# A prologue that loads modulation chunks in pairs, into eight places, and modulates and projects tile by tile

## The chip, the core and the metric

The kernel runs on one core of one Trainium2 chip. The metric is the device time of one execution in microseconds (us); what is compared are medians of several runs. The core has five engines that work side by side and wait for each other by semaphores: TensorE (PE in the profile), VectorE (DVE), ScalarE (ACT), GpSimd (POOL), and SyncE (SP), which here only issues DMAs.

## The reference

Two blocks of two layers each act on 512 tokens of 1024 values; the first block also carries 256 context tokens, so 768 columns in all. The change touches only the start of the first layer of the first block:

```
silu_c = silu(c);  silu_cc = silu(c_ctx)
mod = silu @ ada_w[0] + ada_b[0]          # 6 vectors of 1024: shift1, scale1, gate1, ...
u = rms_norm(h, g_mix[0]) * (1 + scale1) + shift1     # tokens with c, context with c_ctx
q, k, v = split(u @ na_wqkv)              # 16 heads of 64
q, k = rms_norm(q, gain_q), rms_norm(k, gain_k)
y = neighborhood_attention(q, k, v, ...) @ na_wo
```

Everything is float32. Shift1 and scale1 are two of the six vectors; the other four are needed later.

## The kernel before

**Layout.** Tokens stand transposed in SBUF: 8 tiles of 128 features (k = 0 to 7) by 768 columns, 512 tokens (w = 0) and 256 context tokens (w = 1). Weights come from one tensor `stream` in chunks of 128x2048 float32, 1 MB each. A product of float32 precision is made of three matmuls (`mm3`, lines 287 to 289): each operand is split into a high part, made by ScalarE, and a low part, the rest, made for weights by GpSimd (`low_part`, L248, four pieces of 512 columns a chunk) and for activations by VectorE (L547).

**Stages.** The program is a row of stages, each one `nc.Block()` with a program for each engine. At the end of a block all five engines wait for each other, SyncE too; I call the instant at which the next block's first instructions go the boundary.

**The prologue (first block).** SyncE issues the small tensors, the tokens h in two halves, chunks 0 to 3 of the modulation weights into four places, the first attention weight chunk (queries and keys of head pair 0, "qk0") into `w_raw`, and then chunks 4 to 7, each when the place four chunks earlier has been read. Chunks 0 to 3 hold the shift and 4 to 7 the scale, 256 features each. For each chunk TensorE makes rows (`mod_rows`, 8 matmuls, L564), VectorE copies them (`row`, L687) and TensorE turns them into columns (`mod_columns`, 4 matmuls, L571). Meanwhile ScalarE and VectorE make 1/rms of every token (squares L414, sums L433, Ln and Exp L416 and L419). Only with all eight chunks in columns does VectorE add the bias (`mod`) and make the gain (`gsc`); that ends the block. ScalarE and GpSimd split qk0 during it.

**The attention stage (`na_stage`, second block).** SyncE's program begins with the weights of the values ("vv0", two DMAs, L1505), then 24 small DMAs of bias tables (L1513), then the next weight chunk, the queries and keys of head pair 1 ("qk1", L1501). VectorE and ScalarE modulate 16 pieces (8 tiles of 512 columns, 8 of 256; `Apply`: scale L538, high L522, low L547), and TensorE follows tile by tile with the first queries and keys (`qk_first`: 8 tiles, two products each, 48 matmuls of 512 columns). Then come, in program order:

```
TensorE: sums(0,0), qk(0,2), sums(0,1), sums(0,2), values(0,0), values(0,1), values(0,2), scores(0), ...
ScalarE: square(0,0), square(0,1), rstd(0,0), high(vv0), square(0,2), high(qk1), rstd(0,1), rstd(0,2), ...
```

`qk(0,2)` projects the context, `sums` adds squares, `rstd` reads those sums out of PSUM, `high` splits a weight chunk that has landed. All results of projections and sums go in turn through two PSUM banks (`Linear`): result number n may be written when result n-2 has been read. `values(0,0)` is number 6; number 4 is `sums(0,1)`, which `rstd(0,1)` reads. It also needs the low part of vv0 from GpSimd.

Of the kernel before, what the change touches and what calls it, by code (L numbers as in the profile page):

```python
# [495 lines left out]
class Apply:  # L496
# [3 lines left out]
    def __init__(self, m, rstd, tok, gain, shift, tmp, by_columns=False):  # L500
        self.m, self.rstd, self.gain, self.shift, self.tmp = m, rstd, gain, shift, tmp
        self.by_columns = by_columns
        self.items = [(k, a, b, w) for a, b, w in spans(tok) for k in range(KT)]
        self.scaled, self.high, self.low = (m.shared("norm_" + x) for x in ("scaled", "high", "low"))
        for x in ("scaled", "high", "low"):
            m.spent("norm_" + x, len(self.items))

    def ready(self, k, w=0):
        return self.low.at(KT * w + k + 1)
# [14 lines left out]

    def dve(self, dve):
        m = self.m

        def scale(n):
            k, a, b, w = self.items[n]
            if n >= len(self.tmp):  # L530
                dve.wait_ge(*self.low.at(n - len(self.tmp) + 1))
            late = len(self.rstd.shape) == 3
            out, h, rstd = self.place(n), m.h[:, k, a:b], self.rstd if late else self.rstd[:, a:b]
            if late:
                out, h = quarters(out), quarters(h)
            if self.by_columns and w == 0:
                out, h, rstd = columns_as_rows(out), grid(h), grid(rstd)
            dve.scalar_tensor_tensor(out=out, in0=h, scalar=self.gain(k, w), in1=rstd, op0=ALU.mult,  # L538
                                     op1=ALU.mult).then_inc(self.scaled.sem)

        def low(n):
            k, a, b, w = self.items[n]
            dve.wait_ge(*self.high.at(n + 1))
            if self.shift is None:
                ins = dve.tensor_tensor(m.ul[:, k, a:b], self.place(n), m.uh[:, k, a:b].bitcast(F32), ALU.subtract)
            else:
                ins = dve.scalar_tensor_tensor(out=m.ul[:, k, a:b], in0=self.place(n), scalar=self.shift(k, w),  # L547
                                               in1=m.uh[:, k, a:b].bitcast(F32), op0=ALU.add, op1=ALU.subtract)
            ins.then_inc(self.low.sem)

        scale(0)
        for n in range(len(self.items)):
            if n + 1 < len(self.items):
                scale(n + 1)
            low(n)
# [37 lines left out]
def prologue(nc, m):  # L593

    A, D, E = m.A, m.D, m.E
    FIRST = 8
    with ExitStack() as ctx:
# [3 lines left out]
        more = sb("ada_more", [P, 3, CHUNK])  # L601
        landed = m.ada_ring_in = [m.sem(f"ada_ring_in{s}") for s in range(4)]
        slots = [m.raw[:, 1, :]] + [more[:, n, :] for n in range(3)]
        m.vec_in, h_in, rest_in = m.sem("vec_in"), m.sem("h_in"), m.sem("h_rest_in")
        vec_in = m.vec_in
        pmod = m.bank[:, 6, 0:4 * FIRST]
        norm = Norm(m, sb("n_sq", [P, 2, TOK]), sb("n_acc", [P, TOK]), m.rstd, TOK)
        A.plan(["exp_c"] + Norm.act_steps + ["exp_lam", "w0_hi"])
        D.plan(["eps", "zero", "sig1", "sig2", "silu", "sel"] + Norm.dve_steps + ["row0", "row1", "row2", "row3"] +
               ["q1", "q2", "q3", "lam1", "lam2"] + [f"row{c}" for c in range(4, FIRST)] + ["mod", "gsc"])  # L610
        E.plan(["ada0", "ada1", "n_sum", "lamdot"] + [f"ada{c}" for c in range(2, FIRST)] + ["columns"])
        m.G.plan(["w0_lo"])

        with nc.Block() as block:
            @block.sync
            def _(sp):
# [4 lines left out]
                for c in range(FIRST):  # L621
                    if c == 4:
                        sp.dma_start(m.raw[:, 0, :], m.stream[N_ADA]).then_inc(m.first_in, 16)
                    if c >= 4:
                        sp.wait_ge(E.sem, E.at(f"ada{c - 4}"))
# [3863 lines left out]
```

## Time and profile before

| | us |
|---|---|
| three runs | 2732.64, 2738.05, 2738.17 (median 2738.05) |
| span of the profiled execution, first to last instruction | 2732.2 |
| TensorE busy in it | 2622.8 (96%) |
| boundary between prologue and attention stage (first DMA of the stage) | 40.84 |
| first matmul of `values(0,0)` | 69.84 |

The profiled execution has no time of its own in the list of runs; the nearest of the three, 2732.64, is 0.4 us above its span, and the median 5.9 us above. In a timeline a row gives start, duration, engine, line, operation and tiles; a bracket says how long the engine was idle before it and what ended that. A line of a helper stands for all who call it. For DMAs the row gives the issue, and "to landing" the time from the issue until the data are there.

### The profile page before, as it was taken

The page shows a single profiled execution, that of the slowest core. Times are in us where ns is not written, and L with a number is a line of the kernel's source. Part 1 is how long each engine was busy: PE and PEld are TensorE (multiplying, and loading weights), DVE is VectorE, ACT ScalarE, POOL GpSimd, SP SyncE. Part 2 cuts the span into 40 slices and gives each one's busy share as a digit, 9 for nine tenths or more (in the row PEclk, how much of TensorE's full clock was granted, in tenths as well). Part 3 has the DMA queues.
Part 4 walks back from the last instruction along what each step waited for, and adds up shares of the span by engine and source line. Part 5 has one row for each costly group of instructions (what it writes and reads, how often), then busy time and mean ns, then how long its engine had stood idle before and what let it go on. Part 6 is the DMA issues. An engine that isn't in the chain of part 4 may idle for free. (4 is left out here: it accounts for less than half of the span.)

```text
span 2732.2 us, 38254 instructions
## 1 busy us (share of the span) xinstructions
PE 2622.8 (96%) x14748; PEld 2130.9 (78%) x14748; DVE 1546.6 (57%) x2893; ACT 1073.3 (39%) x1864; POOL 875.4 (32%) x651
## 2 busy tenths in 40 slices
PE   6899999999999999999889999999999999999997
PEld 4777786788888888766668888787778888788886
DVE  4434344687777778556664444544556445516555
ACT  4454545422222222565542322344553434542222
POOL 1211121243333333021124444333334333444443
PEclk8999999999999999999999999999999999999999
DMA  6323333223332332110012222322212221222221
GB/s 244 116 79 97 107 99 115 85 96 108 106 107 107 108 108 70 57 47 32 32 47 96 104 92 92 96 66 74 78 47 102 71 85 62 94 93 93 93 93 62
DMA packets 69652, 243.02 MB, mean 89 GB/s; under 512 B 11780, under 2 KB 29700, under 8 KB 49288
## 3 DMA queue, kind: packets, MB, share of 16 engines
q1 hardware_dynamic: 69512, 241.15, 25.8%
q8 instruction: 89, 1.46, 0.2%
q14 instruction: 51, 0.42, 0.0%
HBM read 239.02 MB, written 2.10 MB: 88 GB/s over the span
## 5 line engine op out<-in xcount | busy, mean ns | idle before, releaser
L248 POOL TENSOR_TENSOR w_lo<-w_raw,w_hi 128x512 fp32r<-128x512 f32 x612 | 820.2, 1371 | 1736.7 <-ACT w_hi L241 602.9
L287 PE MATMUL bank<-u_hi,w_hi 128*128 128x512 f32 (+1 forms) x1952 | 731.8, 375 | 10.8 <-DVE u_lo L547 5.0
L289 PE MATMUL bank<-u_hi,w_lo 128*128 128x512 f32 (+1 forms) x1952 | 719.4, 369 | 0.0
L288 PE MATMUL bank<-u_lo,w_hi 128*128 128x512 f32 (+1 forms) x1952 | 718.7, 368 | 0.0
L287 PEld LDWEIGHTS bank<-u_hi,w_hi 128*128 128x128 f32 x1952 | 368.9, 189 | 80.9 <-issue 14.0
L288 PEld LDWEIGHTS bank<-u_lo,w_hi 128*128 128x128 f32 x1952 | 368.9, 189 | 62.2 <-issue 2.5
L289 PEld LDWEIGHTS bank<-u_hi,w_lo 128*128 128x128 f32 x1952 | 368.5, 189 | 62.3
L1052 DVE SCALAR_TENSOR_TENSOR resid<-bank,mod,resid 128x512 f32<-128x512 f32 (+1 forms) x384 | 242.0, 657 | 140.5 <-PE bank L289 136.1
L287 PE MATMUL bank<-hid_hi,w_hi 128*128 128x512 f32 (+1 forms) x768 | 275.5, 359 | 0.0
L289 PE MATMUL bank<-hid_hi,w_lo 128*128 128x512 f32 (+1 forms) x768 | 273.0, 355 | 0.0
L288 PE MATMUL bank<-hid_lo,w_hi 128*128 128x512 f32 (+1 forms) x768 | 272.1, 354 | 0.0
L241 ACT ACTIVATE w_hi<-w_raw 128x2048 fp32r<-128x2048 f32 x64 | 122.7, 1917 | 299.0 <-PE bank L289 298.0
L287 PE MATMUL bank<-w_hi,u_hi 128*128 128x256 f32 (+1 forms) x624 | 193.9, 311 | 5.3 <-POOL w_lo L248 3.0
L763 DVE SCALAR_TENSOR_TENSOR ada_acc<-ada_ring,silu_c,ada_acc 128x256 f32<-128x256 f32 x336 | 195.6, 651 | 0.0
L289 PE MATMUL bank<-w_hi,u_lo 128*128 128x256 f32 (+1 forms) x624 | 190.9, 306 | 0.0
L288 PE MATMUL bank<-w_lo,u_hi 128*128 128x256 f32 (+1 forms) x624 | 190.8, 306 | 0.0
L913 ACT ACTIVATE relu<-bank 128x768 f32<-128x768 f32 (+1 forms) x64 | 45.2, 706 | 319.6 <-PE bank L289 319.6
L289 PEld LDWEIGHTS bank<-hid_hi,w_lo 128*128 128x128 f32 x768 | 144.8, 189 | 23.7
L288 PEld LDWEIGHTS bank<-hid_lo,w_hi 128*128 128x128 f32 x768 | 144.2, 188 | 22.2
L287 PEld LDWEIGHTS bank<-hid_hi,w_hi 128*128 128x128 f32 x768 | 144.1, 188 | 20.8
L1039 DVE TENSOR_TENSOR square<-relu 128x768 f32<-128x768 f32 (+1 forms) x64 | 63.7, 996 | 143.1 <-ACT relu L913 142.9
L287 PEld LDWEIGHTS bank<-w_hi,u_hi 128*128 128x128 f32 x624 | 119.8, 192 | 17.7 <-POOL w_lo L248 4.6
(410 smaller groups left out, 3888.6 us busy)
## 6 DMA issues: line engine op xcount, KB each, us to landing
w_raw<-stream SPq DMA_DIRECT2D x150, 1024.0 KB, 4.9
w_raw<-stream SPq DMA_DIRECT2D x56, 512.0 KB, 4.4
ada_ring<-stream SPq DMA_DIRECT2D x48, 512.0 KB, 4.7
bias<-bias SPq DMA_DIRECT2D x192, 64.0 KB, 2.3
ada_more<-stream SPq DMA_DIRECT2D x6, 1024.0 KB, 13.2
resid<-h SPq DMA_DIRECT2D x2, 1536.0 KB, 8.7
w_raw<-stream SPq DMA_DIRECT2D x8, 256.0 KB, 3.9
out<-resid SPq DMA_DIRECT2D x8, 256.0 KB, 2.0
```

The source lines that it names most:

```text
L241: act.activation(m.wh[:, s, 0:width], m.raw[:, s, 0:width], ACT.Copy).then_inc(m.hi_split, 1)
L248: ins = eng.tensor_tensor(m.wl[:, s, w], m.raw[:, s, w], m.wh[:, s, w].bitcast(F32), ALU.subtract)
L287: pe.matmul(out, lh, rh, start=start, stop=False)
L288: pe.matmul(out, lh, rl, start=False, stop=False)
L289: return pe.matmul(out, ll, rh, start=False, stop=stop)
L763: ins = dve.scalar_tensor_tensor(out=acc, in0=w[:, k, :], scalar=scale, in1=acc, op0=ALU.mult, op1=ALU.add)
L913: act.activation(relu[:, par, t, :], place(g, t)[:, 0:tok], ACT.Relu).then_inc(*A.mark(f"e_{g}{t}"))
L1039: dve.tensor_tensor(square[:, t, :], relu[:, par, t, :], relu[:, par, t, :], ALU.mult).then_inc(*D.mark(f"s_{g}{t}"))
L1052: ins = dve.scalar_tensor_tensor(out=m.h[:, n, a:b], in0=place(g, n)[:, a:b], scalar=m.mod[:, layer, 5, n, w:w + 1], in1=m.h[:, n, a:b], o ...
```

## The change

The eight chunks get a place each (seven in `ada_more`, one in `w_raw`), so SyncE issues all of them without a wait, and in pairs: shift and scale of the same 256 features. The qk0 chunk goes behind the first pair. As soon as a pair is in columns, VectorE makes `mod` and `gsc` for those two tiles and modulates them, with ScalarE, into four buffers `scaled`; TensorE projects their queries and keys. The modulation of all 16 pieces and the whole of `qk_first` thus stand in the prologue's block, and the attention stage begins with `sums(0,0)` on TensorE and `square(0,0)` on ScalarE. SyncE's program of the attention stage is the same. The core of the diff:

```diff
         self.by_columns = by_columns
         self.items = [(k, a, b, w) for a, b, w in spans(tok) for k in range(KT)]
+        if order:
+            self.items = [self.items[KT * w + k] for k, w in order]
+        self.index = {(k, w): n for n, (k, a, b, w) in enumerate(self.items)}
...
         for x in ("scaled", "high", "low"):
             m.spent("norm_" + x, len(self.items))
 
     def ready(self, k, w=0):
-        return self.low.at(KT * w + k + 1)
+        return self.low.at(self.index[k, w] + 1)
 
     def place(self, n):
...
+    def scale(self, dve, n):
+        m = self.m
+        k, a, b, w = self.items[n]
+        if n >= len(self.tmp):
+            dve.wait_ge(*self.low.at(n - len(self.tmp) + 1))
...
     A, D, E = m.A, m.D, m.E
-    FIRST = 8
+    FIRST, QUADS = 8, KT // 2
...
-        more = sb("ada_more", [P, 3, CHUNK])
+        more = sb("ada_more", [P, FIRST - 1, CHUNK])
...
+        chunks = [s * QUADS + q for q in range(QUADS) for s in range(2)]
+        pmod = [m.bank[:, 4 + q, 0:8] for q in range(QUADS)]
...
+        tmp = sb("scaled", [P, 4, LAT])
+        apply = Apply(m, m.rstd, TOK, lambda k, w: m.gsc[:, 0, 0, k, w:w + 1],
+                      lambda k, w: m.mod[:, 0, 0, k, w:w + 1], [tmp[:, n, :] for n in range(4)], by_columns=True,
+                      order=[(2 * q + x, w) for q, w in ((0, 0), (0, 1), (1, 0), (1, 1), (2, 0), (3, 0), (2, 1), (3, 1))
+                             for x in range(2)])
+        m.qk_first_done = m.sem("na_lin_done")
...
-                for c in range(FIRST):
-                    if c == 4:
+                for n, c in enumerate(chunks):
+                    if n == 2:
                         sp.dma_start(m.raw[:, 0, :], m.stream[N_ADA]).then_inc(m.first_in, 16)
-                    if c >= 4:
-                        sp.wait_ge(E.sem, E.at(f"ada{c - 4}"))
-                    sp.dma_start(slots[c % 4], m.stream[c]).then_inc(landed[c % 4], 16)
+                    sp.dma_start(slots[n], m.stream[c]).then_inc(landed[n], 16)
...
                 act.wait_ge(m.first_in, 16)
                 act.activation(m.wh[:, 0, :], m.raw[:, 0, :], ACT.Copy).then_inc(*A.mark("w0_hi"))
+                apply.act(act)
...
+                def columns(q):
+                    if q == 3:
+                        pe.wait_ge(A.sem, A.at("exp_lam"))
+                    for s in range(2):
+                        pe.wait_ge(D.sem, D.at(f"row{2 * q + s}"))
+                        ins = mod_columns(pe, m, pmod[q][:, 4 * s:4 * s + 4], part[:, s, :])
+                    ins.then_inc(*E.mark(f"columns{q}"))
+
+                def qk_first(q):
+
+                    wh, wl = (w[:, 0, :].rearrange("p (k n) -> p k n", k=KT) for w in (m.wh, m.wl))
+                    for k in range(2 * q, 2 * q + 2):
+                        pe.wait_ge(*apply.ready(k))
+                        for p in range(2):
+                            c = slice(p * P, p * P + P)
+                            ins = mm3(pe, m.bank[:, p, :], wh[:, k, c], wl[:, k, c], m.uh[:, k, 0:LAT],
+                                      m.ul[:, k, 0:LAT], k == 0, k == KT - 1)
+                            if k == KT - 1:
+                                ins.then_inc(m.qk_first_done)
...
                 columns(0)
-                for c in range(2, FIRST):
-                    rows(c)
-                    columns(c - 1)
-                columns(FIRST - 1).then_inc(*E.mark("columns"))
+                for q in range(1, QUADS):
+                    rows(2 * q)
+                    rows(2 * q + 1)
+                    columns(q)
+                    if q == 1:
+                        pe.wait_ge(m.G.sem, m.G.at("w0_lo"))
+                    qk_first(q - 1)
+                qk_first(QUADS - 1)
...
+                def row(n):
+                    dve.wait_ge(E.sem, E.at(f"ada{n}"))
+                    if n >= 2:
+                        dve.wait_ge(E.sem, E.at(f"columns{n // 2 - 1}"))
+                    dve.tensor_copy(part[:, n % 2, :], m.bank[:, 2 + n % 2, 0:2 * P]).then_inc(*D.mark(f"row{n}"))
...
+                row(0)
+                row(1)
...
-                for c in range(4, FIRST):
-                    row(c)
-                dve.wait_ge(E.sem, E.at("columns"))
...
+
+                def normed(q, w):
+                    n = apply.index[2 * q, w]
+                    apply.scale(dve, n)
+                    apply.scale(dve, n + 1)
+                    apply.lower(dve, n)
+                    apply.lower(dve, n + 1)
+                for q in range(QUADS):
+                    modulation(q)
+                    normed(q, 0)
+                    if q + 1 < QUADS:
+                        row(2 * q + 2)
+                        row(2 * q + 3)
+                    if q < 2:
+                        normed(q, 1)
+                normed(2, 1)
+                normed(3, 1)
...
-        norm = Apply(m, m.rstd, TOK, lambda k, w: m.gsc[:, 0, 0, k, w:w + 1],
-                     lambda k, w: m.mod[:, 0, 0, k, w:w + 1],
-                     [pt[:, 0, :], pt[:, 1, :], s_sb[:, :, :].rearrange("p h n -> p (h n)")], by_columns=True)
...
-                norm.act(act, 0, KT + 4)
                 square(0, 0)
                 square(0, 1)
-                norm.act(act, KT + 4)
                 rstd(0, 0)
                 high(fills[1])
                 square(0, 2)
...
-                norm.dve(dve)
                 for p in range(QK):
                     normalise_qk(0, p)
                 maximum(0)
...
-                def qk_first():
-
-                    pe.wait_ge(*chunk_lo.at(fill["qk", 0] + 1))
-                    wh, wl = columns(("qk", 0), 0), columns(("qk", 0), 1)
-                    for k in range(KT):
-                        pe.wait_ge(*norm.ready(k))
...
                         for k in range(KT):
-                            if i == 0 and x == 0:
-                                pe.wait_ge(*norm.ready(k, 1))
...
-                qk_first()
                 sums(0, 0)
                 qk(0, 2)
```

TensorE before, in the prologue: rows of one chunk (`ada_more`, or `w_raw` for its place) and columns of the one before (`parts`) in turn.

```order
L564 MATMUL bank<-ada_more,silu_c 32x256 [waits vector_steps,ada_ring_in3]
L564 MATMUL bank<-ada_more,silu_c 32x256 x7
L571 MATMUL bank<-mod_sel,parts 128x2 [waits vector_steps]
L571 MATMUL bank<-mod_sel,parts 128x2
L564 MATMUL bank<-w_raw,silu_c 32x256 [waits vector_steps,ada_ring_in0]
L564 MATMUL bank<-w_raw,silu_c 32x256 x7
L571 MATMUL bank<-mod_sel,parts 128x2 [waits vector_steps]
L571 MATMUL bank<-mod_sel,parts 128x2
```

Each chunk's columns stand behind the next chunk's rows, and nothing else waits between them. TensorE now, from the columns of the second pair on. `gpsimd_steps` is the low part of qk0, `late_norm_low` the low part of a modulated tile, `ada_first_in4` and `5` the landing of the third pair.

```order
L574 MATMUL bank<-mod_sel,parts 128x2 [waits vector_steps]
L574 MATMUL bank<-mod_sel,parts 128x2
L287 MATMUL bank<-u_hi,w_hi 128x512 [waits late_norm_low,gpsimd_steps]
L288 MATMUL bank<-u_lo,w_hi 128x512
L289 MATMUL bank<-u_hi,w_lo 128x512
...
L289 MATMUL bank<-u_hi,w_lo 128x512
L567 MATMUL bank<-ada_more,silu_c 32x256 [waits vector_steps,ada_first_in4]
L567 MATMUL bank<-ada_more,silu_c 32x256 x7
L567 MATMUL bank<-ada_more,silu_c 32x256 [waits vector_steps,ada_first_in5]
L567 MATMUL bank<-ada_more,silu_c 32x256 x7
```

The twelve matmuls of two tiles, and their waits, now stand ahead of the rows of the third pair.

VectorE before, from the first copies of rows (`parts<-bank`) to the first modulated tile (`pt` and `s` are its buffers, `resid` is h):

```order
L687 COPY parts<-bank 128x256 [waits tensor_steps] x4
L692 TENSOR_SCALAR vec_sb<-vec_sb 128x1 x3
L695 TENSOR_TENSOR misc<-lam 128x1 [waits scalar_steps]
L698 TENSOR_SCALAR misc<-misc 128x1 [waits vector_steps]
L687 COPY parts<-bank 128x256 [waits tensor_steps] x4
L704 TENSOR_TENSOR mod<-bank,vec_sb 128x32 [waits tensor_steps]
L708 SCALAR_TENSOR_TENSOR gsc<-mod,vec_sb 128x16 [waits vector_steps]
...
L1697 UNCONDITIONAL_BRANCH [waits barrier_Pool_Activation_PE_DVE_SP_release]
L538 SCALAR_TENSOR_TENSOR pt<-resid,gsc,rstd_first 128x8x64 x2
L547 SCALAR_TENSOR_TENSOR u_lo<-pt,mod,u_hi 128x512 [waits late_norm_high]
```

The modulation followed all eight copies and the boundary. VectorE now, from the first `mod` to the second:

```order
L730 TENSOR_TENSOR mod<-bank,vec_sb 128x2x4 [waits tensor_steps]
L733 SCALAR_TENSOR_TENSOR gsc<-mod,vec_sb 128x4 [waits vector_steps]
L539 SCALAR_TENSOR_TENSOR scaled<-resid,gsc,rstd_first 128x8x64 [waits scalar_steps,vector_steps]
L539 SCALAR_TENSOR_TENSOR scaled<-resid,gsc,rstd_first 128x8x64
L549 SCALAR_TENSOR_TENSOR u_lo<-scaled,mod,u_hi 128x512 [waits late_norm_high] x2
L723 COPY parts<-bank 128x256 [waits tensor_steps] x2
L539 SCALAR_TENSOR_TENSOR scaled<-resid,gsc,rstd_first 128x256 x2
L549 SCALAR_TENSOR_TENSOR u_lo<-scaled,mod,u_hi 128x256 [waits late_norm_high] x2
L730 TENSOR_TENSOR mod<-bank,vec_sb 128x2x4 [waits tensor_steps]
L733 SCALAR_TENSOR_TENSOR gsc<-mod,vec_sb 128x4 [waits vector_steps]
```

The copies of rows (`parts<-bank`) of the second pair now stand behind two modulated tiles.

## Rows read from the trace of the kernel before

**Rows 1.** The page's span; a row of TensorE's waits, 0 to 140 us: total, times, longest.

```profile
span 2732.2 us, 38254 instructions
...
PE bank L287 <- POOL w_lo L248: 1.8, 1, 1.8
```

**Rows 2.** SyncE's timeline: start, us, issuing instructions, line.

```profile
40.84 0.81 SPq L1505 DMA_DIRECT2D w_raw<-stream  x2
41.70 15.31 SPq L1513 DMA_DIRECT2D bias<-bias  x24
57.05 13.10 SPq L1501 DMA_DIRECT2D w_raw<-stream  x2
```

**Rows 3.** Line 1501 from 50 to 62 us, with its DMA's landing.

```profile
L1501 SPq DMA_DIRECT2D w_raw<-stream x1: 591/591/591, 57.0 to 57.0; - x1
...
DMA to landing us min/median/max: 6.0/6.0/6.0
```

**Rows 4.** ScalarE's timeline, 15 to 71 us.

```profile
22.41 0.15 ACT L638 ACTIVATE lam<-bank 128x2 f32<-128x2 f32 x1
...
62.85 1.90 ACT L1577 ACTIVATE w_hi<-w_raw 128x2048 fp32r<-128x2048 f32 x1
...
66.79 1.91 ACT L1577 ACTIVATE w_hi<-w_raw 128x2048 fp32r<-128x2048 f32 x1
68.59 0.69 ACT L1591 ACTIVATE qk_sq<-bank,misc 128x512 f32<-128x512 f32 x1
```

**Rows 5.** TensorE's timeline, 15 to 70 us.

```profile
22.19 0.61 PE L571 MATMUL bank<-mod_sel,parts 128*128 128x2 f32 x4
22.73 1.07 PE L564 MATMUL bank<-ada_more,silu_c 128*32 128x256 f32 x16
...
27.37 1.94 PE L564 MATMUL bank<-w_raw,silu_c 128*32 128x256 f32 x16 [3.04 <-DMA w_raw<-stream]
...
46.00 0.63 PE L289 MATMUL bank<-u_hi,w_lo 128*128 128x512 f32 x1
46.43 0.63 PE L287 MATMUL bank<-u_hi,w_hi 128*128 128x512 f32 x1
...
52.27 0.39 PE L288 MATMUL bank<-u_lo,w_hi 128*128 128x512 f32 x1
52.50 0.39 PE L289 MATMUL bank<-u_hi,w_lo 128*128 128x512 f32 x1
...
69.84 0.38 PE L287 MATMUL bank<-w_hi,u_hi 128*128 128x256 f32 x1 [1.76 <-POOL w_lo L248]
```

**Rows 6.** VectorE's timeline, 38 to 62 us.

```profile
38.39 0.42 DVE L687 COPY parts<-bank 128x256 f32<-128x256 f32 x1 [2.39 <-PE bank L564]
40.16 0.19 DVE L704 TENSOR_TENSOR mod<-bank,vec_sb 128x32 f32<-128x32 f32 x1 [1.35 <-PE bank L571]
...
40.90 2.10 DVE L538 SCALAR_TENSOR_TENSOR pt<-resid,gsc,rstd_first 128x512 f32<-128x512 f32 x2 [0.34 <-PEq L614]
...
59.49 0.49 DVE L547 SCALAR_TENSOR_TENSOR u_lo<-pt,mod,u_hi 128x256 fp32r<-128x256 f32 x1 [1.37 <-ACT u_hi L522]
...
61.74 0.48 DVE L547 SCALAR_TENSOR_TENSOR u_lo<-pt,mod,u_hi 128x256 fp32r<-128x256 f32 x1 [0.18 <-ACT u_hi L522]
```

**Rows 7.** VectorE's timeline, 62 to 76 us.

```profile
62.98 0.75 DVE L1703 SCALAR_TENSOR_TENSOR qk_normed<-qk_normed,vec_sb,qk_sq 128x512 f32<-128x512 f32 x1 [0.76 <-ACT qk_sq L1594]
69.97 1.60 DVE L1703 SCALAR_TENSOR_TENSOR qk_normed<-qk_normed,vec_sb,qk_sq 128x512 f32<-128x512 f32 x1 [6.24 <-ACT qk_sq L1594]
71.50 2.92 DVE L1708 SCALAR_TENSOR_TENSOR qk_normed<-qk_normed,vec_sb,qk_sq 128x256 f32<-128x256 f32 x2
```

**Rows 8.** GpSimd's instructions on w_lo, 63 to 76 us.

```profile
L248 POOL TENSOR_TENSOR w_lo<-w_raw,w_hi x8: 1253/1278/1727, 64.8 to 74.1; 128x512 fp32r<-128x512 f32 x8
```

**Rows 9.** Windows: stretch, length, busy per engine, granted clock, DMA share, GB/s.

```profile
34.00:36.00 2.00, 2.00 (x19) 0.95 (x11) 0.42 (x1) 0.00 (x0) 0.00 (x0) 0.50 0.07 29
70.00:80.00 10.00, 10.00 (x72) 10.00 (x73) 4.42 (x3) 2.50 (x5) 5.57 (x4) 0.83 0.64 203
```

## What is forecast, with its working

> **What bounds the kernel now.** I read the page first: the span is 2732.2 us [rows 1] and TensorE is busy for most of it, so time is won or lost only where TensorE waits or runs at its low clock. The change touches the first 70 us, so I went on to the timelines of the engines there, and then asked of each wait which of its conditions came last. Up to 34 us the stretch is a matter of DMA: in the window from 34 us on only 29 GB/s are left [rows 9], the last chunk is there. Then come copies, columns and `mod` until the boundary at 40.84 [rows 2, 6]; then VectorE modulates 16 pieces until 62.22, with TensorE behind it. The last wait is what counts. `values(0,0)` starts at 69.84, on the low part of vv0 [rows 1, 5]. From there TensorE works through the values without a pause, and everything later hangs on it by semaphores, so I take the shift of that start as the shift of the end. `values(0,0)` has three conditions: TensorE must be through with what is ahead, vv0 must be split, and `rstd(0,1)` must have read its bank. The third was close already: `rstd(0,1)` starts on ScalarE at 68.59 and takes 0.69 [rows 4], 0.6 us before the low part came. It stands behind `high(qk1)`, and that needs the DMA of qk1.
>
> **That DMA hangs on the boundary alone.** SyncE issues vv0 at 40.84, then 24 bias loads in a row, 15.31 us of issuing, and qk1 at 57.05, which is 16.2 after the boundary; it lands 6.0 us later [rows 2, 3], at boundary + 22.2. Before, nobody noticed: ScalarE came to `high(qk1)` at 66.79 [rows 4], boundary + 26.0. If the boundary moves later while the work behind it shrinks, this transfer is what ends last:
>
> values(0,0) = boundary + 22.2 (landing) + 1.8 (`high`, 66.79 to 68.59) + 0.7 (Ln) = boundary + 24.7, against boundary + 29.0 before [rows 4, 5].
>
> So the change saves 4.3 us behind the boundary, all of its earlier projection included, and costs whatever it adds in front. It breaks even with a boundary at 45.1.
>
> **Where the boundary goes.** All 16 pieces now lie in front of it on VectorE, in a block that ends only when the last is done.
> - Start. `mod` of the first pair waits for `lam`, which needs `exp_lam`, done at 22.56 [rows 4]; with the small instructions behind it 22.9.
> - The pieces took 40.90 to 62.22 less waits of 1.37 and 0.18 [rows 6]: 19.8.
> - Six copies of rows at 0.42 [rows 6]: 2.5. Four times `mod` and `gsc`; one pair with its wait took 40.16 to about 40.6 [rows 6], I take 0.5: 2.0.
> - Together 22.9 + 24.3 = 47.2, if VectorE never waited. Even this is behind 45.1.
> - GpSimd. It now splits qk0 while VectorE modulates. That chunk is third in the queue of large ones; in its place before stood one whose rows TensorE made at 22.73 or earlier [rows 5], so it is there when ScalarE comes from `exp_lam`, at 22.6, and is split by 24.5 (1.9 a chunk [rows 4]). GpSimd begins then. Before, no piece of the modulation ran beside GpSimd, but the normalising of queries did: the same instruction took 0.75 alone and 1.60 beside `w_lo`, the two of 256 columns 1.46 each where others take 0.48 [rows 6, 7]. That is 0.85 to 1.0 for each instruction that meets a GpSimd piece. Four pieces meet four: 3.4. GpSimd's pieces stretch as well, from 1.25 to 1.73 [rows 8], so qk0 is split at 24.5 + 4 x 1.73 = 31.4.
> - TensorE. It may start `qk_first` of the first pair at 31.4 only, and the rows of the third pair are queued behind these twelve matmuls. At the low clock one costs 0.43 (46.00 to 46.43), at the high 0.23 [rows 5]. The engine has been mostly idle, so 12 x 0.43 = 5.1, done at 36.5; rows of a chunk cost 1.07 or 1.94 [rows 5]. With the clock up by then they end at 37.6 and 38.7. VectorE, by the sums above, asks for them at about 36.3, and its copies lie between: it waits 2.0. For the last pair it waits for two chunks' columns (2 x 0.61 and the handing over [rows 5]): 1.3. Together 3.3.
> - The boundary itself, from `gsc` to the next block's first instructions: 0.3 [rows 2, 6].
>
> Boundary: 47.2 + 3.4 + 3.3 + 0.3 = 54.2. The last pair's chunks have landed at 34.5 and bind nothing, and `qk_first` of the last pair ends under the context pieces of 256 columns (eight instructions of up to 0.48 [rows 6], over 3 us, against six matmuls at 0.43), so neither adds. At the floor no contention and no waits leave 47.5; at the ceiling TensorE stays at its low clock through the prologue: the middle two `qk_first` cost 2.4 more each, six rows 0.87 more each, the columns 0.8 more a pair, some 11 us, of which most is on the path, since VectorE waits for the rows; boundary 63 to 65.
>
> **The rule on the shared port.** Rows 7 and 8 show both sides stretched. The Trainium skill, page "SBUF — State Buffer", section "Who interferes with whom", says that a VectorE instruction with two SBUF inputs contends with a GpSimd instruction that reads SBUF, and that the loser waits for the whole of the other's instruction. By that rule each of the four pieces would cost VectorE its full 1.25, 5.0 in all, and the boundary would be at 55.8; the trace agrees in kind, with 0.85 to 1.0 a piece.
>
> **The sum.** values(0,0) = 54.2 + 24.7 = 78.9, against 69.84: +9.1. Two small costs: TensorE is idle for some 15 us ahead of it, so the values start at the low clock. In the window of 70 to 80 it already had a mean of 0.83 [rows 9], 3.4 us at half speed, that is 1.7 lost; a second such stretch may come, from 0 to 1.7, I take 0.5. And the next chunk's DMA is now issued right behind qk1 and may slow its landing, from 0 to 1.5; I take 0.4. Nothing is saved in return: the two `sums`, the context projection and splitting vv0 all end by boundary + 14, idle behind the transfer. Forecast +10.0 us: 2742.2 for the profiled span, and on the median, 5.9 above the span, 2738.05 + 10 = 2748.0.
>
> **Rivals.**
> 1. *The clock stays low* through the prologue: boundary 63 to 65 and +19 to +21, 2758. For it: rows took 1.94 at 27.37, and in the window of 34 to 36 us the granted clock was 0.50 although TensorE was busy throughout [rows 5, 9]. Against it: in `qk_first` it rose between 46.4 and 52.3 [rows 5]. Chance 12%.
> 2. *The overlaps cost little*: no contention, short waits, boundary at 48 to 51, +3 to +6, 2742.5. For it: GpSimd may slip into VectorE's waits. Against it: rows 7. Chance 21%.
> 3. *The faster side: qk1 does not bind.* If the transfer of qk1 were hidden after all, the chain by vv0 would decide: landing no later than the 6.0 of rows 3, `high` 1.9 [rows 4], GpSimd 4 x 1.25 [rows 8], thus boundary + 12.9. With 54.2 this gives 67.1, -2.7 us; with 50 it gives -7: 2731 to 2735.3. It decides once qk1 is issued within about 5 us of the boundary instead of 16.2. For it: no engine waited for this DMA in the profile. Against it: ScalarE's order and SyncE's are the same as before, and 24 issues at 0.64 each don't shrink. Chance 6%.
> 4. *The pairs do not land as pairs.* With nine transfers queued at once they could share the engines and land together near 34 us; then VectorE starts its first tile there instead of at 23, boundary about 59, +15: 2753. Against it: with five large ones queued before, the second modulation chunk after the first pair could be used at 22.73, long before the last of them was needed [rows 5]. Chance 4%.
>
> **How the numbers follow.** The forecast has 57%. A change below 0.2%, 5.5 us, cannot be told from none. Slower: nearly all of the forecast (55), all of 1 and 4 (16), a third of 2 (7): 0.79. Same: two thirds of 2, the forecast's tail: 0.15. Faster: 0.06. Range: from case 2 (+3.5, 2741.5) to just short of case 1 (2757). The forecast's own bounds are +7 to +13.
>
> **What would show it.** Right: the block ends near 54 with VectorE last; the qk1 DMA is issued 16.2 later; ScalarE is idle for over 10 us ahead of a `w_hi` that ends in a DMA's landing; TensorE is idle as long ahead of `values(0,0)`, near 79; VectorE instructions near 25 to 31 us are stretched beside `w_lo`; VectorE waits for TensorE at the rows of the third pair. Wrong: `values(0,0)` begins within 15 us of the boundary, or the boundary lies before 47, or later stages differ by more than a microsecond in length.

## The result: 12.8 us slower, and where the profile puts it

| | before | after |
|---|---|---|
| median of four runs each | 2736.86 us (2732.64 to 2738.17) | 2749.64 us (2749.29 to 2750.15) |
| profiled execution | span 2732.2 (time not among the four) | 2749.29, span 2747.5 |
| boundary (next block's first instructions) | 40.84 | 55.76 |
| `values(0,0)` starts | 69.84 | 80.23 |
| first scores | 88.79 | 100.14 |

The ratio is 1.0044, with a 95% interval of 1.0028 to 1.006: slower by 12.0 us by the ratio, 7.7 to 16.4 by the interval. The forecast was +10.0, 2748.0. In every run that has both numbers the time is 1.8 us above the span, so I estimate the profiled execution of before at 2734.0, 2.9 below its median; that of after is 0.4 below its own. The spans therefore differ by more (15.3) than the medians (12.8).

What TensorE waited for from 0 to 140 us in the changed kernel (total us, times, longest):

```profile
PE bank L567 <- DMA w_raw<-stream: 15.2, 1, 15.2
PE bank L287 <- ACT qk_sq L1645: 14.0, 1, 14.0
PE bank L574 <- DVE parts L723: 5.0, 2, 4.0
```

In [rows 1] line 287 waited 1.8 us for GpSimd. It now waits 14.0 us, for ScalarE's Ln of `rstd(0,1)`. The first row is the start of the program, the same in both. ScalarE alone does not explain the second; read from ScalarE back to SyncE. ScalarE's timeline (start, us, instruction, what ended the idle time before it):

```profile
23.41 0.15 ACT L650 ACTIVATE lam<-bank 128x2 f32<-128x2 f32 x1
...
62.12 1.92 ACT L1631 ACTIVATE w_hi<-w_raw 128x2048 fp32r<-128x2048 f32 x1 [2.69 <-DMA w_raw<-stream]
...
77.60 1.91 ACT L1631 ACTIVATE w_hi<-w_raw 128x2048 fp32r<-128x2048 f32 x1 [12.56 <-DMA w_raw<-stream]
79.41 0.67 ACT L1645 ACTIVATE qk_sq<-bank,misc 128x512 f32<-128x512 f32 x1
```

SyncE's timeline:

```profile
55.76 0.80 SPq L1559 DMA_DIRECT2D w_raw<-stream  x2
56.62 15.93 SPq L1567 DMA_DIRECT2D bias<-bias  x24
72.59 1.05 SPq L1555 DMA_DIRECT2D w_raw<-stream  x2
```

These answer to [rows 2, 4]. SyncE's three steps are in the same order as before and nearly as long (15.93 us for the bias loads, against 15.31); what has moved is their start, with the boundary. qk1 is issued at 72.59 and has landed 5.01 us later, when ScalarE, idle for 12.56 us, takes it up; the Ln that line 287 waits for stands right behind.

The cost in front of the boundary is on VectorE's timeline:

```profile
23.86 0.16 DVE L730 TENSOR_TENSOR mod<-bank,vec_sb 128x8 f32<-128x8 f32 x1
...
24.25 2.13 DVE L539 SCALAR_TENSOR_TENSOR scaled<-resid,gsc,rstd_first 128x512 f32<-128x512 f32 x2
26.23 3.37 DVE L549 SCALAR_TENSOR_TENSOR u_lo<-scaled,mod,u_hi 128x512 fp32r<-128x512 f32 x2
...
30.19 2.23 DVE L539 SCALAR_TENSOR_TENSOR scaled<-resid,gsc,rstd_first 128x256 f32<-128x256 f32 x2
...
36.73 0.75 DVE L549 SCALAR_TENSOR_TENSOR u_lo<-scaled,mod,u_hi 128x512 fp32r<-128x512 f32 x1 [0.23 <-ACT u_hi L525]
38.96 0.42 DVE L723 COPY parts<-bank 128x256 f32<-128x256 f32 x1 [1.48 <-PE bank L567]
39.82 0.42 DVE L723 COPY parts<-bank 128x256 f32<-128x256 f32 x1 [0.44 <-PE bank L567]
40.16 0.87 DVE L539 SCALAR_TENSOR_TENSOR scaled<-resid,gsc,rstd_first 128x256 f32<-128x256 f32 x2
...
47.68 0.17 DVE L730 TENSOR_TENSOR mod<-bank,vec_sb 128x8 f32<-128x8 f32 x1 [0.88 <-PE bank L574]
...
54.59 0.88 DVE L549 SCALAR_TENSOR_TENSOR u_lo<-scaled,mod,u_hi 128x256 fp32r<-128x256 f32 x2 [0.18 <-ACT u_hi L525]
```

VectorE is busy nearly throughout and ends the block, at 55.47. Two instructions of 128x512 (line 549) take 3.37 where a single one takes 0.75 later; two of 128x256 (line 539) take 2.23 at 30.19 and 0.87 at 40.16. The slow ones stand beside GpSimd's four pieces, 1.45 to 1.94 each against 1.25 for the shortest in [rows 8]:

```profile
L248 POOL TENSOR_TENSOR w_lo<-w_raw,w_hi x4: 1449/1710/1943, 25.4 to 30.7; 128x512 fp32r<-128x512 f32 x4
```

And TensorE's clock, in windows (stretch, length, busy us and count per engine, granted clock, DMA share, GB/s):

```profile
28.00:34.00 6.00, 3.67 (x12) 3.27 (x13) 5.75 (x10) 1.02 (x2) 4.14 (x3) 0.50 0.99 408
34.00:36.00 2.00, 2.00 (x6) 1.55 (x5) 2.00 (x3) 0.75 (x2) 0.00 (x0) 0.50 0.00 0
40.00:48.00 8.00, 6.99 (x61) 5.13 (x61) 6.61 (x15) 2.36 (x4) 0.00 (x0) 1.00 0.00 1
48.00:56.00 8.00, 6.86 (x23) 5.12 (x22) 6.86 (x13) 3.49 (x7) 0.00 (x0) 0.79 0.00 0
...
70.00:80.00 10.00, 0.00 (x0) 0.00 (x0) 0.00 (x0) 2.40 (x2) 0.42 (x1) 0.50 0.69 249
80.00:90.00 10.00, 9.77 (x61) 9.80 (x62) 4.70 (x3) 3.17 (x7) 5.20 (x4) 0.71 0.35 107
```

The clock is at 1.2 GHz from 28 to 36 us, comes up to 2.4 for the middle of the prologue, and falls once more between 48 and 56 (0.79 in the mean), where VectorE and not TensorE was last. After the idle stretch the values start low again: 0.71 from 80 to 90 us, where [rows 9] have 0.83 from 70 to 80. The values block takes 19.91 us to the scores, against 18.95 before.

### The profile page after: what moved, and what is told of

It is laid out like the page before. It is cut to its first block and busy times, and to the rows that moved or that the text cites. A ratio compares the mean times of both kernels' runs of the same rounds, so it can differ in the third digit from the quotient of the medians.

```text
span 2747.5 us, 38270 instructions
## 1 busy us (share of the span) xinstructions
PE 2620.6 (95%) x14748; PEld 2131.0 (78%) x14748; DVE 1551.4 (56%) x2899; ACT 1072.8 (39%) x1864; POOL 876.9 (32%) x651
## 5 line engine op out<-in xcount | busy, mean ns | idle before, releaser
L288 PEld LDWEIGHTS bank<-hid_lo,w_hi 128*128 128x128 f32 x768 | 144.2, 188 | 22.2
## 6 DMA issues: line engine op xcount, KB each, us to landing
ada_more<-stream SPq DMA_DIRECT2D x7, 1024.0 KB, 21.9
```

The costliest lines, as they stand in the source:

```text
L288: pe.matmul(out, lh, rl, start=False, stop=False)
```

## The experiments

The theory, after the result: two terms and no more. The boundary moves 14.9 us later, and behind it one late transfer, qk1 by way of ScalarE's queue, decides (rival: the lengthened prologue is the whole cost, and the transfer is late but hidden, so that `values(0,0)` would lie there without it). The experiments first take away the transfer's wait, then the parts of the prologue. Where a median stands, that of the kernel before, run on the same chip alongside, is 2736.58 (for a_qk1_early, b_qk1_early, a_split_late and a_more_bias), 2737.78 (for a_one_piece, a_rows_first, a_hoist and a_best) or 2738.21 (for a_late_ctx, b_places and b_more_bias). The changed kernel was measured beside none of them; so between groups, and against the changed kernel, the ratios to before are the better guide, and the steps in the profile better still.

### 1. The load of qk1 ahead of the bias: a_qk1_early and b_qk1_early

```
     load(fills[1])
+    load(fills[2])
     load_bias(0, 0, bias_in)
     ...
-    for n in range(2, 5):
+    for n in range(3, 5):
```

The same edit on SyncE, made to the changed kernel and to the one before.

> The changed kernel, with SyncE issuing the qk1 load right behind vv0, ahead of the 24 bias loads. My theory (the qk1 transfer, queued behind the bias loads, ends last): it now lands within 9 us of the boundary, ScalarE no longer idles 12.6 us, and values(0,0) starts at boundary + 13 to 14, near 69 instead of 80.2; the time falls by 11 to 12 us, to 2738, the level of the kernel before. Rival (the loss sits in front of the boundary or in the clock, and the idle behind it only takes up what something else would cost): the time falls by less than 3 us.

> The kernel before with qk1 issued ahead of the bias loads. My theory: no gain, within 0.5 us at values(0,0) (69.8), since ScalarE came to the split of qk1 only 26 us after the boundary, later than the landing at 22; the time stays at 2732 to 2738. If an early qk1 load were a gain of its own, it would be 3 us or more faster.

Measured: a_qk1_early 2734.89 (ratio to before 0.9997, 0.9988 to 1.0006), that is 14.7 us less than the changed kernel in the medians and 12.9 by the ratios; b_qk1_early 2736.37 (1.0000, 0.9988 to 1.0011). SyncE and ScalarE of a_qk1_early:

```profile
53.97 0.80 SPq L1559 DMA_DIRECT2D w_raw<-stream  x2
54.82 0.42 SPq L1555 DMA_DIRECT2D w_raw<-stream  x1
55.29 16.12 SPq L1567 DMA_DIRECT2D bias<-bias  x24
```

```profile
61.29 1.91 ACT L1632 ACTIVATE w_hi<-w_raw 128x2048 fp32r<-128x2048 f32 x1 [3.43 <-DMA w_raw<-stream]
65.62 1.91 ACT L1632 ACTIVATE w_hi<-w_raw 128x2048 fp32r<-128x2048 f32 x1 [1.00 <-DMA w_raw<-stream]
```

and its first matmul of the values:

```profile
68.27 0.39 PE L287 MATMUL bank<-w_hi,u_hi 128*128 128x256 f32 x1 [2.47 <-POOL w_lo L248]
```

The wait of 14.0 is gone, with it the whole loss, and TensorE waits for GpSimd again. The same edit does nothing in the kernel before, where the transfer had slack. `values(0,0)` stands 14.3 us after the boundary instead of 24.5; that is 10.2 of the 12.0 us by which it comes earlier, and the other 1.8 are a boundary at 53.97 that the edit has no part in. Without the late transfer the longer prologue is made good by the shorter stage behind it. The run also prices crowding: with vv0 and qk1 in flight together, vv0 is taken up 7.3 us after the boundary, against 6.4 in the changed kernel, so about 1 us.

### 2. The transfer as late, ScalarE's order other: a_split_late

```
     square(0, 2)
-    high(fills[2])
     rstd(0, 1)
     rstd(0, 2)
+    high(fills[2])
```

> The changed kernel, SyncE as it is, but ScalarE splits qk1 behind rstd(0,1) and rstd(0,2) instead of ahead of them. My theory: qk1 lands as late as before (boundary + 22) but nobody on the path waits for it; values(0,0) near 69, time 2738 to 2739. If the transfer itself were the matter (the DMA queue blocked for vv0 or the bias tables too), values(0,0) would stay near 80 and the time at 2749.

Measured: 2736.69 (0.9998, 0.9989 to 1.0008). ScalarE and TensorE:

```profile
61.48 1.92 ACT L1631 ACTIVATE w_hi<-w_raw 128x2048 fp32r<-128x2048 f32 x1 [2.73 <-DMA w_raw<-stream]
77.41 1.91 ACT L1631 ACTIVATE w_hi<-w_raw 128x2048 fp32r<-128x2048 f32 x1 [9.01 <-DMA w_raw<-stream]
```

```profile
68.48 0.39 PE L287 MATMUL bank<-w_hi,u_hi 128*128 128x256 f32 x1 [1.46 <-POOL w_lo L248]
```

qk1 is still issued at 71.95 and ScalarE still waits 9.01 us for it; but nobody needs it yet. The boundary is at 55.08, the values start 13.4 us behind it, and the time is that of a_qk1_early within the runs' spread. So the link was the queue: `rstd(0,1)`, which frees a bank for the values, stood behind a split that it has nothing to do with.

### 3. A longer row of issues: a_more_bias and b_more_bias

```
     load(fills[1])
+    for r in range(GRID_H):
+        sp.dma_start(spare[r:P:GRID_H, :], m.in_bias[0, 0:16, 0:LAT]).then_inc(spare_in, 16)
     load_bias(0, 0, bias_in)
```

Eight loads more, of a tile that nothing reads.

> The changed kernel with eight more small loads (32 KB each, into a tile that nobody reads) ahead of the 24 bias loads. My theory: each issue of about 0.6 us delays qk1 and with it everything, so values(0,0) starts 4.5 to 5.3 us later, near 85, and the time rises by 5 us to 2754.5. Rival (the issue time is not what counts): no change.

> The kernel before with eight more small loads ahead of the bias loads. In the changed kernel the same edit moved values(0,0) by 4.6 us. By my account the kernel before had 3.8 us of slack between the landing of qk1 (boundary + 22.2) and ScalarE's coming to it (+ 26.0), and 0.6 us more until the low part of vv0: a delay of 5.3 us leaves 1 us at values(0,0), and 1 us of time, not distinguishable. If qk1 had been binding already, the full 5 us would show.

Measured: a_more_bias 2755.52 (1.0055, 1.0037 to 1.0074), 5.9 us more than the changed kernel in the medians and 3.0 by the ratios, whose intervals overlap (its four runs range over 10.6 us), so that the profile has to decide; b_more_bias 2738.19 (1.0003, 0.9992 to 1.0014). SyncE of a_more_bias, then SyncE of b_more_bias:

```profile
55.87 5.88 SPq L1589 DMA_DIRECT2D spare<-bias  x8
61.80 15.21 SPq L1568 DMA_DIRECT2D bias<-bias  x24
77.05 1.06 SPq L1556 DMA_DIRECT2D w_raw<-stream  x2
```

```profile
42.04 5.04 SPq L1535 DMA_DIRECT2D spare<-bias  x8
47.12 15.89 SPq L1514 DMA_DIRECT2D bias<-bias  x24
63.06 7.39 SPq L1502 DMA_DIRECT2D w_raw<-stream  x2
```

Each issue costs 0.63 to 0.74 us of SyncE. In the changed kernel qk1 stands 22.0 after the boundary instead of 16.8, and `values(0,0)` 29.8 instead of 24.5: the 5.2 us of issuing come through as 5.4. In the kernel before, qk1 is issued 21.9 after the boundary, 5.7 later than in [rows 2], and the values begin at boundary + 29.8 instead of + 29.0: the first 4.9 us are swallowed. That slack is the 4.3 us between boundary + 24.7 and boundary + 29.0, and the 0.6 beyond it is the landing: ScalarE takes qk1 up 5.3 us after its issue, where [rows 3] have 6.0.

### 4. The prologue's parts: a_one_piece and a_rows_first

a_one_piece: GpSimd makes one of the four pieces of qk0's low part, and VectorE sets the rest to constants early.

```
+    for x in range(1, 4):
+        dve.tensor_copy(m.wl[:, 0, x * LAT:x * LAT + LAT], m.cst[:, 0:LAT])
     ...
-    low_part(pool, m, 0).then_inc(*m.G.mark("w0_lo"))
+    low_part(pool, m, 0, CHUNK // 4).then_inc(*m.G.mark("w0_lo"))
```

> The changed kernel, but GpSimd makes only one of the four pieces of qk0's low part in the prologue (the other three are filled with constants by VectorE early on, so the output is not the reference's). If VectorE and GpSimd hold each other up as rows 7 and 8 show, the VectorE instructions near 25 to 31 us go back to 1.0 and 0.75 us, the boundary comes 3 to 4 us earlier than 55.8, near 52.3, and since everything behind it hangs on the boundary, values(0,0) and the time fall by the same, to 2746. If there is no contention on the path, the boundary moves by less than 1 us.

Measured: 2746.48 (1.0031, 1.0019 to 1.0042), 3.2 us less than the changed kernel, with overlapping intervals. VectorE's timeline:

```profile
24.52 0.15 DVE L732 TENSOR_TENSOR mod<-bank,vec_sb 128x8 f32<-128x8 f32 x1
...
26.88 2.37 DVE L549 SCALAR_TENSOR_TENSOR u_lo<-scaled,mod,u_hi 128x512 fp32r<-128x512 f32 x2
...
29.84 0.86 DVE L539 SCALAR_TENSOR_TENSOR scaled<-resid,gsc,rstd_first 128x256 f32<-128x256 f32 x2
...
31.69 0.16 DVE L732 TENSOR_TENSOR mod<-bank,vec_sb 128x8 f32<-128x8 f32 x1
```

From the first `mod` to the second it takes 7.17 us, against 9.54 in the changed kernel (23.86 to 33.40): three pieces less are 2.4 us less. The one that is left stretches its two neighbours by 0.95 (2.37 against 1.42 for a pair alone: 0.67 from one start to the next and 0.75), so all four cost 3.3. The changed kernel's own rows give the same: 3.37 less 1.42 and 2.23 less 0.87 are 3.3. The expectation had 3 to 4 us for three pieces and the boundary near 52.3. It comes at 54.10, only 1.7 earlier: the 2.4 are there, but this kernel's `mod` also began 0.66 later. Its first chunk landed 0.96 later (TensorE's first matmul at 16.11 against 15.15), and whether the extra copies had a part in that was not tested. That the median met the expected 2746 is therefore luck: `values(0,0)` moved by 1.2 us (79.00 against 80.23), the median by 3.2.

a_rows_first: ScalarE's order of experiment 2, and TensorE's queue as follows.

```
     columns(0)
+    rows(2)
+    rows(3)
     for q in range(1, QUADS):
-        rows(2 * q)
-        rows(2 * q + 1)
         columns(q)
+        if q + 1 < QUADS:
+            rows(2 * q + 2)
+            rows(2 * q + 3)
```

> The changed kernel with the late split of qk1, and TensorE's rows of the next pair put ahead of the twelve matmuls of qk_first instead of behind them. If the waits of VectorE for these rows (1.48 and 0.44 us at the third pair) and for the last pair's columns (0.88) are what the queue on TensorE costs, the boundary comes 2 to 3 us earlier, near 53, and the time falls from 2736.7 by 2, to 2734.5. If VectorE's own work is all that counts, nothing moves.

Measured: 2735.89 (0.9996, 0.9987 to 1.0005), against 2736.69 with the order of experiment 2 alone: in this measurement no difference, and in the profile one of about 1 us. VectorE's timeline:

```profile
37.33 0.75 DVE L726 COPY parts<-bank 128x256 f32<-128x256 f32 x2
...
40.12 0.17 DVE L733 TENSOR_TENSOR mod<-bank,vec_sb 128x8 f32<-128x8 f32 x1 [0.20 <-PE bank L574]
...
45.81 0.17 DVE L733 TENSOR_TENSOR mod<-bank,vec_sb 128x8 f32<-128x8 f32 x1 [0.88 <-PE bank L574]
```

The waits of 1.48 and 0.44 for the third pair's rows are gone; 0.20 and 0.88 for columns stay. The boundary is at 54.03, 1.05 earlier than in a_split_late, where 2 to 3 were expected, and the values start at 67.57 instead of 68.48.

### 5. The loads ahead of the boundary: a_hoist and a_best

a_hoist is a_rows_first with the loads of vv0 and qk1 issued by SyncE inside the first block, as soon as their places are free. a_best is a_hoist with `high(vv0)` inside it too, on ScalarE between two pieces of the modulation.

```
+    sp.wait_ge(E.sem, E.at("ada0"))
+    for p in range(2):
+        sp.dma_start(m.raw[:, 1, p * KT * P:(p + 1) * KT * P], ...).then_inc(m.vv0_in, 16)
+    sp.wait_ge(m.G.sem, m.G.at("w0_lo"))
+    sp.dma_start(m.raw[:, 0, :], m.stream[N_ADA + 3]).then_inc(m.first_in, 16)
     ...
-    apply.act(act)
+    apply.act(act, 0, 10)                                   # a_best only, and the next three
+    act.wait_ge(m.vv0_in, 32)
+    act.activation(m.wh[:, 1, :], m.raw[:, 1, :], ACT.Copy).then_inc(*A.mark("w1_hi"))
+    apply.act(act, 10)
```

> a_rows_first with the loads of vv0 and qk1 issued by SyncE in the prologue, as soon as their places in w_raw are free, instead of behind the boundary. vv0 is then there at the boundary, ScalarE splits it at boundary + 3.3 and not + 6.3, GpSimd ends at + 10.3, and values(0,0) starts there instead of + 13.4: 3 us earlier, 2731.5. If the idle of TensorE ahead of the values has another cause, no gain over a_rows_first.

> a_hoist, and ScalarE splits vv0 still in the prologue, in its idle time ahead of the last pair. GpSimd can begin at the boundary; values(0,0) is then bound by TensorE's own queue (context projection and sums), at boundary + 9.5 to 10: up to 0.8 us earlier than in a_hoist if the 1.9 us split hides in ScalarE's idle time, nothing or a loss of 1 to 2 us if it delays the last pieces. Forecast 2731.

Measured: a_hoist 2733.20 (0.9982, 0.9972 to 0.9991); a_best 2731.37 (0.9982, 0.9973 to 0.9990). Both beat the kernel before by 4.9 us by the ratios (in the medians 4.6 and 6.4), and a_best the changed one by 18 in the medians. GpSimd and TensorE of a_hoist, then of a_best:

```profile
60.57 5.01 POOL L248 TENSOR_TENSOR w_lo<-w_raw,w_hi 128x512 fp32r<-128x512 f32 x4 [28.42 <-ACT w_hi L1640]
...
66.71 0.58 PE L287 MATMUL bank<-w_hi,u_hi 128*128 128x256 f32 x1
```

```profile
54.11 4.96 POOL L248 TENSOR_TENSOR w_lo<-w_raw,w_hi 128x512 fp32r<-128x512 f32 x4 [21.85 <-POOLq L629]
```

```profile
65.49 0.58 PE L287 MATMUL bank<-w_hi,u_hi 128*128 128x256 f32 x1
```

In a_hoist the values start 0.9 us earlier than in a_rows_first, where 3 were expected. The low part of vv0 is ready at 65.58 and no longer waited for; what stands ahead now is TensorE's own work, the context projection and the sums. In a_best GpSimd splits vv0 the moment the boundary falls, and the values start 11.4 us after it instead of 12.6. But a_hoist did not wait for that split either, and both have the boundary at 54.1: the 1.2 us lie in the projection, which ran at a granted clock of 0.57 from 54 to 62 us in a_hoist and of 0.79 in a_best. So the split inside the prologue is not shown to win anything; the ratios of the two kernels are the same, and that a_best met its 2731 was not by the way expected (values at boundary + 9.5 to 10). What both show is the worth of the loads ahead of the boundary, with ScalarE's and TensorE's other order. Left are the boundary and TensorE's queue.

### 6. A shorter prologue: a_late_ctx

a_best with the last four pieces of the context modulated behind the boundary.

```
     apply.act(act, 10, 12)              # ScalarE, first block; likewise VectorE
     ...
+    norm.act(act, 12)                   # ScalarE, next block
     ...
+    for n in range(12, 16):             # VectorE, next block
+        norm.scale(dve, n)
+    for n in range(12, 16):
+        norm.lower(dve, n)
```

> a_best with the last four context pieces (tiles 4 to 7) modulated behind the boundary instead of in front of it. If the boundary is what holds all the rest and VectorE is idle behind it (4.9 us between the last piece and the first normalising in the runs so far), it comes 3.7 us earlier, near 50.3, the pieces lie beside TensorE's and ScalarE's work, and values(0,0) starts 3 us earlier than in a_best, near 62.5; time 2728.5. If the context projection has to wait for them, the gain is under 1 us.

Measured: 2733.23 (0.9986, 0.9977 to 0.9995), 1.9 us more than a_best in the medians and 1.1 by the ratios, whose intervals overlap: at least no gain, where 2728.5 was expected. The values start at 66.28, 0.8 later than in a_best, where the expectation had 62.5. VectorE's timeline:

```profile
52.22 2.95 DVE L539 SCALAR_TENSOR_TENSOR pt<-resid,gsc,rstd_first 128x256 f32<-128x256 f32 x2 [2.43 <-PEq L630]
55.09 1.50 DVE L539 SCALAR_TENSOR_TENSOR s<-resid,gsc,rstd_first 128x256 f32<-128x256 f32 x1
56.52 1.48 DVE L539 SCALAR_TENSOR_TENSOR e<-resid,gsc,rstd_first 128x256 f32<-128x256 f32 x1
```

and a row of TensorE's waits, 40 to 140 us:

```profile
PE bank L287 <- DVE u_lo L549: 2.9, 2, 2.4
```

Two things the expectation had left out. VectorE is through with its part at 49.8 and then waits 2.43 us: the boundary now hangs on TensorE's last `qk_first`, and comes at 52.18, 1.9 earlier and not four. And the scaling of the four moved pieces lands beside GpSimd's splitting of vv0: 1.48 to 1.53 each, where 0.47 is usual. Of TensorE's 2.9 us of waiting 2.4 are for the first moved piece. The overlap that the prologue got rid of was bought again behind it.

### 7. The eight places alone: b_places

The kernel before with eight places for the modulation's chunks and no waits of SyncE for a free place, nothing else changed.

```
-    more = sb("ada_more", [P, 3, CHUNK])
+    more = sb("ada_more", [P, 7, CHUNK])
     ...
-    if c >= 4:
-        sp.wait_ge(E.sem, E.at(f"ada{c - 4}"))
-    sp.dma_start(slots[c % 4], m.stream[c]).then_inc(landed[c % 4], 16)
+    sp.dma_start(slots[c], m.stream[c]).then_inc(landed[c], 16)
```

> One part of the change alone: the kernel before with a place for each of the eight chunks, SyncE issuing all of them without a wait, order and everything else as before. DMA is full up to 34 us either way and TensorE, at its low clock, works off rows and columns behind it, so only the wait of 0.5 us for the seventh chunk can go: boundary 0 to 0.5 us earlier, time within 1 us. If the places were worth something themselves, the boundary would come 2 us or more earlier.

Measured: 2738.10 (1.0000, 0.9991 to 1.0009). The boundary is at 40.97 and the values start at 69.91, as in [rows 2, 5] within 0.2. The places themselves neither win nor lose anything; the new order of the loads, in pairs and with qk0 third, was not run alone.

## Why the forecast was right, step by step

The forecast had two steps, where the boundary goes and what follows behind it, and each part of them can be set beside its row. All numbers are of the changed kernel's profile, those of the second table from the rows above it.

| the boundary | forecast | measured |
|---|---|---|
| first `mod` | 22.9 | 23.86 |
| VectorE's own work | 24.3 | 24.1 (the rest) |
| beside GpSimd | 3.4 | 3.3 (experiment 4) |
| waits for TensorE | 3.3 | 2.8 (1.48 + 0.44 + 0.88) |
| waits for ScalarE | not priced | 1.4 (seven, 0.18 to 0.23) |
| handing over | 0.3 | 0.3 |
| boundary | 54.2 | 55.8 |

| behind it | forecast | measured |
|---|---|---|
| qk1 issued | +16.2 | +16.8 |
| landed | +22.2 | +21.8 |
| `values(0,0)` | +24.7 | +24.5 |

**The mechanism** is shown from three sides: the wait goes when the load comes earlier, it goes when the load is as late but ScalarE does not stand behind it, and it grows by 5.4 when the load is made 5.2 later. The slack of the kernel before, which made the forecast's break-even of 45.1, is shown by b_more_bias.

**Sizes that were off** lie in the boundary, 1.6 us. The start is late by 1.0: in front of `lam` TensorE makes the sum of squares, which took 2.39 us for four matmuls where it took 1.56 in the profile of before, and `lam` came at 23.41 instead of 22.41. That is not the change's doing: over all thirteen profiles `lam` falls anywhere from 21.98 (a_qk1_early) to 24.16 (b_qk1_early), in both kernels, with the sum taking 1.56 to 2.39. The forecast took it from one execution, and so knew it to about 1 us only. The three other kernels whose prologue is the changed one have the boundary at 53.97, 55.02 and 55.08. The term that was missing is ScalarE's 1.4: with only two pieces in turn instead of a long row, VectorE comes to the low part before ScalarE has the high one, once for the tokens and once for the context of a pair, seven times in all. Rows of before had the sign of it, 0.18 at the end of [rows 6], and I counted that as a wait to be left out.

**The two small costs.** The clock was priced at 0.5 and took 0.96 (19.91 against 18.95 us for the values block). Crowding by the next chunk was priced at 0.4, and the landing was not slower but faster (5.0 against 6.0). In all the values start 10.4 later, where the sum had 9.1, and the scores 11.35, where it had 10.0. That these lie as near as they do is in part luck: 2.9 us too little (start 1.0, ScalarE 1.4, clock 0.5) stand against 1.4 too much (VectorE's own work, GpSimd and TensorE 0.8, the stretch behind the boundary 0.2, crowding 0.4).

**The rest of the 12.8.** The medians differ by 12.8 and the spans by 15.3, while the first scores differ by 11.35. From the values on both programs have the same 14480 matmuls in the same order, and yet the lag of a given matmul grows, in a few short stretches. The forecast had named later stages that differ by more than a microsecond as a sign of being wrong, and that sign came. Part of it is the clock. The window around 475 us, first of before, then of after:

```profile
455.00:490.00 35.00, 31.72 (x243) 22.55 (x244) 21.40 (x63) 15.22 (x45) 4.94 (x4) 0.90 0.38 137
```

```profile
455.00:490.00 35.00, 28.68 (x221) 19.18 (x221) 16.88 (x49) 17.76 (x47) 4.99 (x4) 0.85 0.37 124
```

A mean of 0.90 against 0.85 over 35 us is 7 against 10.5 us at half speed, 1.75 us more lost; the lag of a given matmul goes from 10.6 to 13.1 us across this place, and is 15.3 at the end. Waits are in it too: behind 110 us TensorE is idle for 73.6 us, against 68.1 before. But this is not the change's doing for certain: b_places, whose values start at 69.91 like those of before, has 0.85 there too, and its lag behind the profile of before goes from -0.1 to 2.4 us at this place and to 7.7 at the end (span 2739.9). The kernel before itself ranges over 10.6 us from run to run in the first group (2732.43 to 2743.01). The interval, 7.7 to 16.4 us, holds both 11.35 and 12.8; more than that the runs do not say, and whether a later boundary makes such stretches likelier stays open.

**The rivals.** The clock staying low through the prologue (forecast: boundary 63 to 65) did not happen: it was back at 2.4 GHz by 40 us (granted 1.00 from 40 to 48). Overlaps that cost little did not happen either, they cost 6.1 us (3.3 beside GpSimd and 2.8 waiting for TensorE). That qk1 would not bind is refuted by experiment 1, and its price was right in kind: once the load stands at the front, the values start at boundary + 14.3, which is the 12.9 of that rival's chain with 1.3 more for the landing (7.3 against 6.0) and 0.1 between its steps. That the pairs would land together is refuted by the first `mod`, at 23.86. And the rule of the Trainium skill, page "SBUF — State Buffer", section "Who interferes with whom", that the loser waits for the whole of the other's instruction, would have made the four pieces cost 5.0: measured 3.3, 0.8 a piece. The page says "for the whole instruction" of VectorE's 2-port modes, and of two SBUF inputs only that they contend; taken over to these, it is right in kind and above the measurement in size.

## What to carry to other kernels

Work pulled ahead of a point at which all queues start anew delays everything issued behind that point, loads above all: before such a change, find the first transfer behind it, count the issues that stand ahead of it in its queue, and move it first. Ask of each wait of a queue whether the instruction behind it needs what it waits for; here one line's place on ScalarE was worth as much as the load's (experiments 1 and 2). And where one engine's work is moved away from another's, look at what stands in the new place: the same contention was met twice.

## What the runs showed of the hardware

- Many small loads cost SyncE time to issue: 24 loads of 64 KB took it 15.2 to 16.2 us, 0.63 to 0.68 each, in all thirteen profiles, though in those of before and after each landed 2.2 us behind its issue in the median. A load of 1 MB was issued in 0.42 to 0.59; qk1, issued behind them, landed 5 to 6 us later.
- A VectorE instruction of line 549 or 539 beside GpSimd's `TENSOR_TENSOR` was stretched by about 1 us in both sizes: 128x512 from 0.75 to 1.69 in the mean (3.37 for two), 128x256 from 0.47 to between 1.48 and 1.53. The one already running when GpSimd began kept its length (1.13 us in the changed kernel), and it was GpSimd's first piece that was stretched most, from 1.25 to 1.94; the others took 1.45 to 1.71. Copies out of PSUM beside it kept their 0.41.
- TensorE had the low clock of 1.2 GHz (0.50 granted) from 28 to 36 us, though from 34 us on it was busy all the time, and again over 70 to 80 us, idle.
- When the clock falls and rises differs from one execution to the next: the same four matmuls of line 425 took 1.56 to 2.39 us over the thirteen profiles, and the same projection behind the boundary ran at a granted clock of 0.57 in a_hoist and 0.79 in a_best.
